# Row sums of the second output projection moved into its end, and one barrier instead of two at each stage joint, in a 25-stage fp32 transformer kernel

## The reference

```python
def rmsnorm(x, g):
    y = x * lax.rsqrt(jnp.mean(x * x, axis=-1, keepdims=True) + EPS_2)
    return y * g

def swiglu_2(x, w_gate, w_up, w_down):
    return (jax.nn.silu(x @ w_gate) * (x @ w_up)) @ w_down

for i in range(DEPTH):                       # DEPTH = 2
    h = h + 0.5 * swiglu_2(rmsnorm(h, ffn1_norm[i]), ...)
    u = rmsnorm(h, mix_norm[i]) @ w_in[i]
    ...                                      # latent attention, mLSTM, Fourier mixer
    h = h + y @ w_out[i]                     # the second output projection
    h = h + 0.5 * swiglu_2(rmsnorm(h, ffn2_norm[i]), ...)
    gate = sigmoid(rmsnorm(h, ple_gate_norm[i]) @ ple_w_gate[i])
    h = h + gate * rmsnorm(p[i] @ ple_w_proj[i], ple_post_norm[i])
return rmsnorm(h, final_norm)
```

## Time and profile before

| | |
|---|---|
| median of three runs | 3615.33 us |
| the profiled execution, its own time | 3615.63 us |
| its span in the trace | 3613.8 us |
| TensorE matmul busy | 3528.2 us (98%) |
| VectorE, ScalarE, GpSimd busy | 1574.0, 1279.9, 453.7 us |
| granted TensorE clock, mean over the span | 0.993 of full speed |
| DMA | 292.07 MB, mean 81 GB/s |

### The profile page before, as it was taken

How to read it: one execution, slowest core, us unless ns; L and a number is a source line. 1 busy time by engine, 2 the same in 40 slices (tenths; PEclk the granted TensorE clock), 3 DMA queues, 4 the chain that set the end, 5 groups by cost and what they waited for, 6 DMA issues and landing times. The chain is left out here.

```text
span 3613.8 us, 41926 instructions
## 1 busy us (share of the span) xinstructions
PE 3528.2 (98%) x15764; PEld 2772.3 (77%) x15764; DVE 1574.0 (44%) x2129; ACT 1279.9 (35%) x1792; POOL 453.7 (13%) x372
## 2 busy tenths in 40 slices
PE   9999999999999999999999999999999999999998
PEld 7787788877778886888775688877888775678885
DVE  3386433346643334333365733335333365733335
ACT  4243422245542224332333533235332333533324
POOL 0001111000111101221000122102221000022102
PEclk9999999999999999999999999999999999999999
DMA  4201233222123322333220223313333220123322
GB/s 146 86 1 36 76 99 108 96 70 70 38 79 99 104 94 64 99 96 106 80 65 14 71 93 98 113 60 96 99 96 106 79 77 18 53 93 97 112 70 76
DMA packets 78030, 292.07 MB, mean 81 GB/s; under 512 B 8656, under 2 KB 11472, under 8 KB 77648
## 3 DMA queue, kind: packets, MB, share of 16 engines
q1 hardware_dynamic: 77328, 289.31, 25.0%
q10 hardware_dynamic: 576, 1.05, 0.1%
HBM read 288.22 MB, written 2.10 MB: 80 GB/s over the span
## 5 line engine op out<-in xcount | busy, mean ns | idle before, releaser
L146 DVE TENSOR_TENSOR w_low<-w_raw,w_high 128x1024 fp32r<-128x1024 f32 (+4 forms) x513 | 675.1, 1316 | 1524.9 <-ACT w_high L141 1524.9
L180 PE MATMUL bank<-x_high,w_high 128*128 128x512 f32 x2856 | 1121.4, 393 | 22.1 <-DVE w_low L146 9.2
L181 PE MATMUL bank<-x_low,w_high 128*128 128x512 f32 x2856 | 1112.7, 390 | 0.0
L182 PE MATMUL bank<-x_high,w_low 128*128 128x512 f32 x2856 | 1112.5, 390 | 0.0
L141 ACT CAST w_high<-w_raw 128x1024 fp32r<-128x1024 f32 (+4 forms) x513 | 554.9, 1082 | 850.0 <-PE bank L182 841.2
L180 PEld LDWEIGHTS bank<-x_high,w_high 128*128 128x128 f32 x2856 | 537.2, 188 | 146.0 <-DVE w_low L146 13.9
L181 PEld LDWEIGHTS bank<-x_low,w_high 128*128 128x128 f32 x2856 | 537.4, 188 | 112.8 <-issue 2.2
L182 PEld LDWEIGHTS bank<-x_high,w_low 128*128 128x128 f32 x2856 | 536.9, 188 | 112.0
L180 PE MATMUL bank<-hidden_high,w_high 128*128 128x512 f32 x1056 | 410.8, 389 | 0.0
L181 PE MATMUL bank<-hidden_low,w_high 128*128 128x512 f32 x1056 | 410.8, 389 | 0.0
L182 PE MATMUL bank<-hidden_high,w_low 128*128 128x512 f32 x1056 | 410.8, 389 | 0.0
(11 more groups left out here) (529 smaller groups left out, 3446.7 us busy)
## 6 DMA issues: line engine op xcount, KB each, us to landing
w_raw<-in_stream SPq DMA_DIRECT2D x381, 512.0 KB, 3.5
w_raw<-in_stream SPq DMA_DIRECT2D x96, 704.0 KB, 4.0
w_raw<-in_stream SPq DMA_DIRECT2D x16, 384.0 KB, 3.1
w_raw<-in_stream SPq DMA_DIRECT2D x4, 576.0 KB, 3.7
dft_positions<-in_dft SPq DMA_DIRECT2D x2, 1024.0 KB, 4.8
w_raw<-in_stream SPq DMA_DIRECT2D x16, 128.0 KB, 2.1
out<-result SPq DMA_DIRECT2D x4, 512.0 KB, 2.7
h<-in_x ACTq DMA_DIRECT2D x4, 256.0 KB, 6.4
```

Of the source, the lines that this page charges most:

```text
L146: self.nc.vector.tensor_tensor(self.lo[:, j % 2, 0:size], self.raw[:, j % RAW_SLOTS, 0:size], self.hi[:, j % 2, 0:size].bitcast(F32), ALU. ...
L180: nc.tensor.matmul(out, lhs[0], rhs[0], start=start, stop=False)
L181: nc.tensor.matmul(out, lhs[0], rhs[1], start=False, stop=False)
L182: return nc.tensor.matmul(out, lhs[1], rhs[0], start=False, stop=stop)
```

## The change

`stage` no longer ends with a clear and a barrier. It puts its semaphores on a list, and the next `stage`, after allocating its own from those that are free, has GpSimd clear the listed ones in front of its part of the next Block. So each joint has the Block's own barrier alone; the other engines do not wait for the clear. After the last stage the clear and one barrier are kept.

In `second_out_stage` the squares get four buffers in place of two. GpSimd adds tiles 0 to 3 only (3 additions for 6). TensorE runs 6 constant matmuls for 24, and then multiplies `sq_sum` and the squares of tiles 4 to 7, each with a wait of its own, into bank 4. `rms_ffn_stage` takes as `summed` the bank in which the sums stand (4 after the output projection, 6 in the first layer's first use), and has TensorE count `row_sums` at its start in place of the two matmuls.

```diff
+STALE = []
+
+def clear_stale(nc):
+    if STALE:
+        nc.clear_and_free_semaphores(list(STALE))
+        STALE.clear()
+
 @contextmanager
 def stage(nc, names):
     sems = [nc.alloc_semaphore(f"{n}_{nc.next_id()}") for n in names.split()]
+    clear_stale(nc)
     yield namedtuple("Stage", names)(*sems)
-    nc.clear_and_free_semaphores(sems)
-    nc.all_engine_barrier()
+    STALE.extend(sems)
...
-def rstd_chain(nc, C, act, S):
+def rstd_chain(nc, C, act, S, bank):
     act.wait_ge(S.row_sums, 1)
-    nc.scalar.activation(C.rstd[:, :], C.bank[6][:, :], ACT.Ln, bias=C.eps[EPS_2]).then_inc(S.logged, 1)
+    nc.scalar.activation(C.rstd[:, :], bank[:, :], ACT.Ln, bias=C.eps[EPS_2]).then_inc(S.logged, 1)
...
@@ second_out_stage
-    sq, rs, squares = prj[:, 5:7, :], C.sq, C.ring[:, 0:2, :]
+    sq, rs, squares = prj[:, 5:7, :], C.sq, C.ring
+    square_at = [squares[:, t, :] for t in (0, 1, 0, 1, 2, 3)] + [C.sq_last[:, :], squares[:, 0, :]]
...
                 pe.wait_ge(S.residual_done, 1)
-                keep_warm(nc, C, C.bank[0], 24)
+                keep_warm(nc, C, C.bank[0], 6)
+                pe.wait_ge(S.residual_done, SUM_BANK + 1)
+                pe.wait_ge(S.sq_added, 3)
+                nc.tensor.matmul(C.bank[SUM_BANK][:, :], C.ones_mean, C.sq_sum[:, :], start=True, stop=False)
+                for t in range(4, DT):
+                    pe.wait_ge(S.squared, t + 1)
+                    nc.tensor.matmul(C.bank[SUM_BANK][:, :], C.ones_mean, square_at[t], start=False, stop=t == DT - 1)
...
                     act.wait_ge(S.residual_done, t + 1)
-                    after.act_squares(nc, C, act, S, 0, t, squares)
+                    after.high(nc, C, act, S, t)
+                    if t in (2, 3):
+                        act.wait_ge(S.sq_added, 1)
+                    elif t == DT - 1:
+                        act.wait_ge(S.sq_added, 2)
+                    nc.scalar.activation(square_at[t], C.h[:, t, :], ACT.Square).then_inc(S.squared, 1)
...
             def _(pool):
-                for t in range(DT - 1):
+                for t in range(4):
                     after.pool_adds(nc, C, pool, S, t, squares)
...
@@ second_layer
-    rms_ffn_stage(nc, C, 0.5, after=Handover(rms(C, "ple_gate_norm", L)), p_dram=C.p_dram[L, :, :, :])
+    rms_ffn_stage(nc, C, 0.5, summed=SUM_BANK, after=Handover(rms(C, "ple_gate_norm", L)), p_dram=C.p_dram[L, :, :, :])
...
@@ program
         final_norm_stage(nc, C, out)
+        clear_stale(nc)
+        nc.all_engine_barrier()
```

More of the change, by code:

```diff
@@ L283 @@
 LN_TABLE, LN_EXP_TABLE = 5, 6
+SUM_BANK = 4
 def centred(C, t):
@@ L881, in ffn_stage, with rms_ffn_stage @@
     W.base += jobs
-def rms_ffn_stage(nc, C, scale, gain=None, summed=False, after=None, p_dram=None):
+def rms_ffn_stage(nc, C, scale, gain=None, summed=None, after=None, p_dram=None):
     W = C.W
@@ L963, in up @@
                     if is_first(k, u):
-                        rstd_chain(nc, C, act, S)
+                        rstd_chain(nc, C, act, S, C.bank[summed or 6])
                     if u % 2 == 0:
@@ L3244, in second_layer @@
 def second_layer(nc, C, L):
-    rms_ffn_stage(nc, C, 0.5, gain=rms(C, "ffn1_norm", L), summed=L == 0,
+    rms_ffn_stage(nc, C, 0.5, gain=rms(C, "ffn1_norm", L), summed=None if L else 6,
                   after=Handover(rms(C, "mix_norm", L)))
```

## The result

The changed kernel takes 3592.41 us, the median of four runs (3591.04 to 3597.53), against 3614.99 us for the kernel before in the same comparison: a ratio of 0.9937, 95% interval 0.9925 to 0.995. The profiled execution took 3591.04 us, its span is 3589.3 us.

What follows compares the result with a forecast made beforehand. TensorE, busy 98% of the span, was taken as the bound. Terms of 13.1, 3.4 and 1.8 us sum to 18.3 us, off the median of 3615.33 us: 3597.0 us, with an 8-in-10 range of 3591 to 3603 us.

Steps and rivals of the forecast that it cites:

- Term 1, the joints: At 24 joints, one barrier less, with GpSimd's drain and clear off the path: 0.55 us each, 13.1 us.
- From about 1.0 to 0.45: Sign at each joint: TensorE's idle time falls from about 1.0 to 0.45 us; 24 joints together give 13 us.
- The clear at nothing: GpSimd's clear in front of its own work costs nothing; uncovered, a stage gives back at most 0.3 to 0.7 us.
- Term 2, the sums: In two feed-forward stages behind output projections, TensorE drops two fp32 sum matmuls: 1.7 us each, 3.4 us.
- Term 3, the projection's end: Output projection ends 1.1 us earlier with fewer GpSimd additions, TensorE last; net 0.9 us after the new count, twice: 1.8 us.
- the clock holds where it fell: Rival: TensorE's low-clock stretches go as idle time at joints halves; some 6 us more, 3591 us, chance 0.12.
- main forecast: The whole kernel at 3597.0 us, with its own range 3594 to 3600 us; chance 0.68.
- two stretches in the mLSTM and output stages: Low-clock stretches of TensorE in these stages that could go, at 1.0 to 1.5 us each.
- Those at the layer norms: Three low-clock stretches of TensorE at layer norms that could go, at 1.0 to 1.5 us each.
- Code late behind a single barrier: Rival: code or GpSimd late at half the joints, 3603.6 us, chance 0.05; at all joints, 3610 us, chance 0.03.
- The clock falls at more places: Rival: everything shifts in time and three more low-clock stretches come at 1.5 us each; 3601.5 us, chance 0.11.
- slower: Rival: the clock falls at nearly every joint, 1.5 us each; 3624 us at 18 joints, chance 0.01.

Runs made afterwards that it cites:

- the idle additions: The changed kernel with three GpSimd additions more at the end of the output projection, into a tile that nothing reads; 3597.11 us.
- the two-sums kernel: The changed kernel with two buffers, six GpSimd additions and 24 constant matmuls as before, and two sums at the output projection's end; 3598.94 us.
- the last one: The changed kernel with constant matmuls filling TensorE's waits in the second input projection, the linear-attention block and the layer-norm stage; 3592.55 us.

## Why the prediction was right, and where its size was off

*Term 1, the joints: right.* Predicted 13.1 us; 13.4 both as the median of the joints alone, where the clock has a part, and as the sum of the stretches between the two releases. The anatomy holds too: 0.33 us for the barrier's steps (0.3 predicted), the rest for drain and clear. "From about 1.0 to 0.45" was right at the mean: over the 19 joints where TensorE waits for little but the barrier, its idle time went from 1.02 to 0.46 us, at the first from 1.01 to 0.30.

*The clear at nothing: right.* A microsecond more of GpSimd at every joint moved almost no stage. The reason given, that GpSimd "starts no later than before", was wrong in four stages: in the second mLSTM stage its first instruction comes 1.45 us behind the Block's release, where it was 0.66. Nothing there waited for it.

*Term 2, the sums: right.* The stages behind the projections were to lose 1.5 us besides the joint; they lost 1.5 and 1.7 in the kernel with old joints and new sums. TensorE's new count costs 0.12 us (its first weight load comes 0.53 us behind the release, before 0.41), against 0.15 to 0.2.

*Term 3, the projection's end: right in every step.* The constant matmuls, ten passes of 0.43 us, TensorE last and VectorE 1.0 us ahead of it, the split at 1.2 us: all as written. VectorE ends 2.0 to 2.1 us earlier in the stage against 2.3, and the stage became 1.2 us shorter against 1.1. That VectorE was held up by GpSimd is shown by the idle additions, which bring 1.6 us of it back.

*The sum: 18.3 predicted, 19.0 from the two halves measured alone,* and 18.9 from the rows at full clock (13.4 of the joints, 5.5 of the four stages). The difference to 22.6 is where the prediction fell short: "I put no term in" for the clock. The prediction offered the rival *the clock holds where it fell*, at 3591 us and a chance of 0.12, and this is nearest to what came. The stated range held because it took in this rival: the main forecast's own 3594 to 3600 does not reach the median, and only two of the nine runs, both at the lowest mean clock, lie in it. Its places were half right. Of "two stretches in the mLSTM and output stages" both are gone in every new trace (likely by the shorter joints, as said above); at 1.55 and 0.6 us two falls of the one and three of the other make 4.9 us over the four old traces, 1.2 us a run. Those at the layer norms cost far less than the 1.2 us I gave them: a trace with 6.8 us of low clock there and one with 3.4 differ by 0.02 us behind the first two and by 0.4 behind the third. The layer-norm stage itself is another matter: 10.68 us with 3.4 us of low clock and 11.98 with 6.8, in the two traces of the changed kernel. Not foreseen were the input projections, where the clock fell in 8 of 8 cases before and in 9 of 14 with the new joints. There the trigger is a 3 us wait inside the stage, 100 us away from a joint, as filling it shows; at 1.4 us a fall the difference is worth an estimated 1.0 us a run. Why it fell less often with new joints is open, and so is the last microsecond or two of the 22.6.

*Code late behind a single barrier: did not happen.* The first instructions follow the release by 0.07 to 0.29 us, at each joint as before, and the instruction queue has 83 packets in both traces. (They take 1.1 us each; the prediction's 1.4 came from the rounded share.) The page that stood behind this rival (the Trainium skill, Advanced Engine Details and Errata, ISA Cache) says that the instruction cache has only two lines. No run here shows the lines; no joint showed a fetch in its way. *The clock falls at more places* and *slower* did not come in the changed kernel, though its relatives did fall at new places: the two-sums kernel and the last one in the Fox attention, at some 3 us, and the new joints alone behind the projection, at 1.6.

## What to carry to other kernels

Where TensorE is busy 98% of the time, look at what all engines do at a joint. Here an empty barrier cost 0.33 us and a clear in front of one 0.23, so bookkeeping belongs behind the release, on the engine that is needed last. Ask of each helper on GpSimd whom it slows, not only whether it is in time: three additions there made VectorE 1.6 us later and the stage 0.9 us longer. And compare traces stage by stage at equal clock; the same stage then repeated within a few hundredths of a microsecond here, so changes of half a microsecond can be read from single traces while medians still move by 2 or 3.

## What was not expected of the hardware

- All runs of the kernel before, in every comparison, lie between 3611.6 and 3616.5 us, while the new joints alone spread from 3597.2 to 3606.5. Within one kernel each 0.001 of mean clock goes with some 2 us; between kernels it does not, since the cost depends on where the clock falls.
- TensorE's clock fell after an idle time of about 3 us in the middle of a stage, and one such fall cost 1.4 us in a stage of 116, or 2.7 where it lasted 6.8 us. At the start of the first feed-forward stage a fall of 3.4 us cost nothing measurable (374.80 us with the new joints alone, 374.79 in the changed kernel, whose clock held there): TensorE waits there for VectorE's `x_low`, for 0.85 us in the one and 1.49 in the other.
- Freed semaphores that are reused in another order split one clear into up to six, and each piece has a drain of its own: 0.13 us together at the median. With one piece they end 0.2 to 0.5 us behind the release, with five or six up to 1.4.
